# Gate rows of the second block computed as a weight-stationary tile, keys spread by TensorE

## The reference

```python
def hybrid_layer(x, ...):
    h = rmsnorm(x, norm_mix)
    z = h @ w_in                                   # 512 x 1024 times 1024 x 4360
    q_a, k_a, v_a, q_m, k_m, v_m, o_m, if_m, gates = split(z)
    # q_a: 8 heads of 64, k_a and v_a: 2 heads of 64, q_m, k_m: 4 heads of 64,
    # v_m, o_m: 4 heads of 128, if_m: 2 x 4 columns, gates: 2048 columns
    q_a, k_a = partial_rope(rmsnorm(q_a)), partial_rope(rmsnorm(k_a))
    att = sliding_window_attention(q_a, k_a, v_a, sinks)
    i_pre, f_pre = split(if_m + m_gate_bias)       # 4 heads each, 512 tokens
    hm = mlstm_chunkwise(q_m, k_m, v_m, i_pre, f_pre)
    hm = rmsnorm(hm) * sigmoid(o_m)
    mixed = sigmoid(g_a) * (att @ w_att_branch) + sigmoid(g_m) * (hm @ w_m_branch)
    x = x + mixed @ w_out
    u = relu(rmsnorm(x, norm_ffn) @ w_ff1)
    return x + (u * u) @ w_ff2
```

## Time and profile before

| | |
|---|---|
| median of three runs | 3104.98 us |
| the profiled execution | 3104.98 us |
| its span, first to last instruction | 3103.3 us |
| TensorE busy | 3045.1 us, 98% |
| VectorE busy | 1562.1 us, 50% |
| ScalarE busy | 1133.7 us, 37% |
| mean granted TensorE clock | 0.992 |
| ticks 26 to 39 of the second block's first layer | 1761.5 to 1803.6 us |
| the same ticks of its second layer | 2469.2 to 2513.0 us |

### The profile page before, as it was taken

The page is one execution under the profiler, slowest core; times in us unless marked ns, Lnnn a source line. Parts: engine busy times, 40 slices in busy tenths (PEclk is TensorE's granted clock), DMA queues, the critical chain, the costliest instruction groups (busy, mean ns, idle before and its releaser), DMA issues.

```text
span 3103.3 us, 39594 instructions
## 1 busy us (share of the span) xinstructions
PE 3045.1 (98%) x16998; PEld 2549.7 (82%) x16998; DVE 1562.1 (50%) x2145; ACT 1133.7 (37%) x1673; POOL 30.3 (1%) x44
## 2 busy tenths in 40 slices
PE   7999999999999999999999999999999999999999
PEld 6788888887987777888888777898889877798887
DVE  7776654545255465533325654653344654653342
ACT  5555421224233333432224455432232355433231
POOL 0000000000000000000000000000000000000000
PEclk9999999999999999999999999999999999999999
DMA  7433355542332222132322222223222222223322
GB/s 283 156 123 109 109 181 172 168 135 68 95 95 68 69 69 69 46 104 95 95 89 81 82 68 68 82 86 101 98 95 89 82 69 68 82 86 101 99 95 82
DMA packets 219917, 311.59 MB, mean 100 GB/s; under 512 B 12032, under 2 KB 120544, under 8 KB 219744
## 3 DMA queue, kind: packets, MB, share of 16 engines
q1 hardware_dynamic: 208528, 267.01, 26.7%
q0 software_dynamic: 10880, 41.95, 3.8%
q10 hardware_dynamic: 336, 0.12, 0.0%
HBM read 306.93 MB, written 2.10 MB: 100 GB/s over the span
## 4 chain that ended last, share of the span: by engine, by line
PE 88%; DVE 8%; ACT 2%; DMA 1%; issue 1%; ACTq 0%; SPq 0%; DVEq 0%; POOLq 0%
PE G L2065 62%; PE G L2108 8%; PE G L2069 6%; DVE yT L1586 1%; PE X L2161 1%; PE X L2427 1%; DVE w_lo L1235 1%; PE G L2087 1%; PE X L2504 1%; PE G L2227 1%; DMA ada_raw<-in_ada_w 1%; PE X L2488 1%; PE X L2511 1%; DVE hT L1372 1%; DVE yT L1367 1%
## 5 line engine op out<-in xcount | busy, mean ns | idle before, releaser
L2065 PE MATMUL G<-u_hi,w_hi 128*128 128x512 f32 x2160 | 865.5, 401 | 3.3 <-issue 3.2
L2065 PE MATMUL G<-u_hi,w_lo 128*128 128x512 f32 x2160 | 842.7, 390 | 0.0
L2065 PE MATMUL G<-u_lo,w_hi 128*128 128x512 f32 x2160 | 841.3, 389 | 0.0
L1235 DVE TENSOR_TENSOR w_lo<-raw,w_hi 128x2048 fp32r<-128x2048 f32 (+3 forms) x242 | 544.9, 2253 | 501.6 <-ACT w_hi L638 501.0
L638 ACT CAST w_hi<-raw 128x2048 fp32r<-128x2048 f32 (+3 forms) x242 | 454.5, 1880 | 531.8 <-DMA raw<-in_w_ff 242.3
L2065 PEld LDWEIGHTS G<-u_hi,w_hi 128*128 128x128 f32 x2160 | 405.4, 188 | 108.5 <-issue 25.5
L2065 PEld LDWEIGHTS G<-u_hi,w_lo 128*128 128x128 f32 x2160 | 405.4, 188 | 87.8
L2065 PEld LDWEIGHTS G<-u_lo,w_hi 128*128 128x128 f32 x2160 | 406.1, 188 | 79.7 <-issue 1.4
L2065 PE MATMUL G<-ff_hi,w_hi 128*128 128x512 f32 x448 | 174.9, 390 | 0.0
L2065 PE MATMUL G<-ff_hi,w_lo 128*128 128x512 f32 x448 | 174.4, 389 | 0.0
L2065 PE MATMUL G<-ff_lo,w_hi 128*128 128x512 f32 x448 | 174.3, 389 | 0.0
(11 more groups left out here) (425 smaller groups left out, 4341.0 us busy)
## 6 DMA issues: line engine op xcount, KB each, us to landing
raw<-in_w_ff SPq DMA_DIRECT2D x128, 512.0 KB, 4.4
raw<-in_ffn_w_in SPq DMA_DIRECT2D x88, 512.0 KB, 4.5
ada_raw<-in_ada_w POOLq DMA_DIRECT2D x40, 1024.0 KB, 7.2
raw<-in_w_in SPq DMA_DIRECT2D x56, 512.0 KB, 4.4
raw<-in_attn_w_in SPq DMA_DIRECT2D x96, 256.0 KB, 3.7
raw<-in_ffn_w_out SPq DMA_DIRECT2D x40, 512.0 KB, 4.8
raw<-in_hgrn_w_in SPq DMA_DIRECT2D x32, 512.0 KB, 4.7
raw<-in_attn_w_in SPq DMA_DIRECT2D x24, 512.0 KB, 4.5
```

The costliest lines, as they stand in the source:

```text
L1235: tt(w_lo[slot][:, 0:nk, 0:w], raw[slot][:, 0:nk, 0:w], w_hi[slot][:, 0:nk, 0:w].bitcast(F32), ALU.subtract).then_inc(s_lo, 1)
L2065: ins = mm(G[0:c1_ - c0, m, :], w[iw][:, k, c0:c1_], xs[ix][:, x0(b) + kk, :], start=first, stop=last, skip_group_check=True)
```

## The change

The eight `if` columns leave block b = 3, which now has 384 columns, and form the fourth tile of block b = 4. Its weights are 36 columns: i in columns 0 to 3, f in 32 to 35, between them columns of the next matrix part that are computed and not used. So PE makes the two groups of rows directly, in ticks 35 and 39, and the four transposes, the buffer `z_ift`, its clearing by DVE and ACT's copies into it are gone.

The keys are spread by PE: at tick 22 two products with a selecting constant `selk` write both key heads into two banks of PSUM, and ACT copies them at tick 24 in one instruction. PE waits for `k_rotated` at tick 22, ACT for the new `k_spread`. The constant is one more DMA of 128 KB at the start of `at_v` in the first block.

The exponentials stay where they are, in rows, and PE turns i and two exponentials back with three products of 4 columns for each of four token tiles, in place of one product of 68 columns. DVE copies the result in one instruction.

```diff
+    sel = []
+    for kv in range(2):
+        sel.append((r[:, None] // 64 == kv) & (r[:, None] % 64 == r[None, :] % 64))
+    g["selk"] = np.concatenate(sel, 1)
...
         Z_COLUMNS = (z_run((Z["q_a"], 512)), z_run((Z["k_a"], P), (Z["o_m"], P), (Z["q_m"], 256)), z_run((Z["k_m"], 512)),
-                     z_run((Z["v_m"] + 256, 256), (Z["v_a"], P), (Z["if"], 2 * M_HEADS)), z_run((Z["o_m"] + P, 3 * P)))
+                     z_run((Z["v_m"] + 256, 256), (Z["v_a"], P)), z_run((Z["o_m"] + P, 3 * P + GATE_AT)) + [(3 * P + GATE_AT, Z["if"] + M_HEADS, M_HEADS)])
...
                     sp.dma_start(sel4[:, :], a["con2"][:, where2["sel4"][0]:where2["sel4"][1]]).then_inc(s_con, 16)
+                    sp.dma_start(flat(selk[:, :, :]), a["con2"][:, where2["selk"][0]:where2["selk"][1]]).then_inc(s_con, 16)
...
                 elif T == 24:
-                    n.take(ws["k_rotated"])
+                    n.take(ws["k_spread"])
                     n.take(ws["q_scaled"])
-                    for kv in range(2):
-                        for a_ in range(2):
-                            ins = sc.copy(tmp[64 * a_:64 * a_ + 64, kv, :], z_k[64 * kv:64 * kv + 64, 0, :])
-                    n.give(ins, ws["k_ready"])
+                    n.give(sc.copy(tmp[:, 0:2, :], X[:, 0:2, :]), ws["k_ready"])
...
                     n.take(ms["rows"])
-                    sc.copy(cosT[32:32 + M_HEADS, :], z_if[:, 0, :])
-                    sc.activation(cosT[64:64 + M_HEADS, :], row[1], ACT.Exp)
-                    sc.activation(cosT[96:96 + M_HEADS, :], row[3], ACT.Exp, scale=-1.0)
+                    sc.activation(row[1], row[1], ACT.Exp)
                     sc.activation(row[0], row[0], ACT.Exp)
+                    sc.activation(row[3], row[3], ACT.Exp, scale=-1.0)
...
-                            lambda: sc.copy(z_v[:, m, :], G[:, m, 256:256 + P]),
-                            lambda: sc.copy(z_ift[:, m, :].rearrange("p (i c) -> p i c", i=2)[:, :, 0:M_HEADS],
-                                            G[:, m, 3 * P:3 * P + 2 * M_HEADS].rearrange("p (i h) -> p i h", i=2)))
+                            lambda: sc.copy(z_v[:, m, :], G[:, m, 256:256 + P]))
...
                     n.take(ms["columns"])
-                    for i in range(3):
-                        v.tensor_copy(mcol[:, 16 * i:16 * i + 16].rearrange("p (j h) -> p j h", j=TB),
-                                      X[:, 0, 0:272].rearrange("p (j c) -> p j c", j=TB)[:, :, 32 * i:32 * i + M_HEADS])
-                    n.give(v.tensor_copy(mcol[:, 48:80], X[:, 0, 272:304]), ms["columns_copied"])
+                    n.give(v.tensor_copy(mcol[:, :], X[:, 0, 0:80]), ms["columns_copied"])
...
-                    v.memset(z_ift[:, :, :], 0.0)
...
+                elif T == 22:
+                    n.take(ws["k_std"])
+                    n.take(ws["k_rotated"])
+                    for kv in range(2):
+                        ins = mm(X[:, kv, :], selk[:, kv, :], z_k[:, 0, :], start=True, stop=True)
+                    n.give(ins, ws["k_spread"])
...
                 for j in range(TB):
-                    mm(X[:, 0, 68 * j:68 * j + 68], cosT[:, blk(j)], ident[:, 32:100], start=j == 0, stop=True, skip_group_check=True)
+                    mm(X[:, 0, 4 * j:4 * j + 4], gi[:, blk(j)], ident[0:4, 0:4], start=j == 0, stop=True, skip_group_check=True)
+                    mm(X[:, 0, 16 + 4 * j:20 + 4 * j], row[1][:, blk(j)], ident[0:4, 0:4], start=False, stop=True, skip_group_check=True)
+                    mm(X[:, 0, 64 + 4 * j:68 + 4 * j], row[3][:, blk(j)], ident[0:4, 0:4], start=False, stop=True, skip_group_check=True)
...
-                    return [(m, (0, 3 * P + 2 * M_HEADS), (0, 3 * P + 2 * M_HEADS))]
-                return gate_rows if (b, m) == (4, 3) else None
-
-            def gate_rows():
-
-                for j in range(TB):
-                    ins = tr(G[0:GATE_AT + M_HEADS, 3, blk(j)], z_ift[:, j, 0:GATE_AT + M_HEADS], ident)
-                return ins
+                    return [(m, (0, 3 * P), (0, 3 * P))]
+                return (3 * P, 3 * P + GATE_AT + M_HEADS) if (b, m) == (4, 3) else None
```

More of the change, by code:

```diff
@@ L42 @@
 SLOTS = 3
-GATE_AT = 32
 def constants():
@@ L217, in build @@
             cosT, sinT = sb("cosT", [P, S], F32, room), sb("sinT", [P, S], F32, room)
-            sel4, z_ift = sb("sel4", [P, 512], F32, room), sb("z_if_by_token", [P, TB, 2 * GATE_AT], F32, room)
+            sel4, selk = sb("sel4", [P, 512], F32, room), sb("selk", [P, 2, P], F32, room)
         ada_raw = sb("ada_raw", [P, 2, 4, 512])
@@ L294, in build @@
                                              "output", "squares", "variance", "std", "normed", "transposed", "done")}
-        ws = {k: sem("window_" + k) for k in ("q_squares", "k_squares", "q_sums", "k_sums", "q_std", "k_std", "q_scaled", "q_rotated", "k_rotated", "k_ready",
+        ws = {k: sem("window_" + k) for k in ("q_squares", "k_squares", "q_sums", "k_sums", "q_std", "k_std", "q_scaled", "q_rotated", "k_rotated", "k_spread", "k_ready",
                                               "scores", "maximum", "weights", "normalized", "transposed", "copied", "output", "done", "sinks")}
@@ L1643, in rope_tables @@
             def rope_tables():
-                n.take(s_con, 48)
+                n.take(s_con, 64)
                 two_pi = 2 * np.pi
@@ L1843, in mlstm @@
                         bank, i = m_bank(c)
-                        ins = stt(m_state[:, c, :], m_state[:, c - 1, :], mcol[:, 48 + 8 * h + c:49 + 8 * h + c],
+                        ins = stt(m_state[:, c, :], m_state[:, c - 1, :], mcol[:, 32 + 8 * h + c:33 + 8 * h + c],
                                   X[:, bank, (P + 1) * i:(P + 1) * (i + 1)], ALU.mult, ALU.add)
@@ L1853, in mlstm @@
                     link(tt(stat[:, 4:8], den, stat[:, 0:4], ALU.max))
-                    link(tt(stat[:, 4:8], stat[:, 4:8], mcol[:, 32 + h:48:4], ALU.max))
+                    link(tt(stat[:, 4:8], stat[:, 4:8], mcol[:, 64 + h:80:4], ALU.max))
                     link(stt(stat[:, 8:12], stat[:, 4:8], EPS, stat[:, 4:8], ALU.mult, ALU.mult))
@@ L2046, in plain @@
                         last_k = g["ktiles"] - 1
-                        if spec is gate_rows:
-                            if s == g["chunks"] - 1:
-                                ins = gate_rows()
-                                ins.then_inc(s_tile, 1)
-                            else:
-                                ins.then_inc(s_inner, 1)
-                            continue
                         for part in (spec if isinstance(spec, list) else [None]):
@@ L2516, in gate_columns @@
                     return
+                gi = z_if[:, 0, :]
                 n.take(ms["rows_exp"])
@@ L2519, in gate_columns @@
                 for j in range(TB):
-                    mm(X[:, 0, 68 * j:68 * j + 68], cosT[:, blk(j)], ident[:, 32:100], start=j == 0, stop=True, skip_group_check=True)
+                    mm(X[:, 0, 4 * j:4 * j + 4], gi[:, blk(j)], ident[0:4, 0:4], start=j == 0, stop=True, skip_group_check=True)
+                    mm(X[:, 0, 16 + 4 * j:20 + 4 * j], row[1][:, blk(j)], ident[0:4, 0:4], start=False, stop=True, skip_group_check=True)
+                    mm(X[:, 0, 64 + 4 * j:68 + 4 * j], row[3][:, blk(j)], ident[0:4, 0:4], start=False, stop=True, skip_group_check=True)
                 for h in range(M_HEADS):
-                    ins = mm(X[:, 0, 272 + 8 * h:280 + 8 * h], sel4[0:4, blk(h)], srow[:, 6, :], start=False, stop=True, skip_group_check=True)
+                    ins = mm(X[:, 0, 32 + 8 * h:40 + 8 * h], sel4[0:4, blk(h)], srow[:, 6, :], start=False, stop=True, skip_group_check=True)
                 n.give(ins, ms["columns"])
```

1 line of the change is left out of this document (added).

## The result

The changed kernel took 3124.07 us (median of 4 runs, 3123.41 to 3126.72), the kernel before 3105.25 us beside it (4 runs): ratio 1.0062, with a 95% interval of 1.0049 to 1.0075. It is slower by 18.8 us. The forecast was 3118.8 us with a range up to 3123.5, so the direction was right and the time lies outside the range, by 0.6 us. On another chip the same kernel took 3119.36 us against 3106.55, ratio 1.0046 (1.0033 to 1.006); that time lies inside the range. Both intervals hold 1.005, about 15.5 us.

A forecast was written before the change was run, and what follows sets the result against it. TensorE (PE), busy for 98% of the span, was taken as the bound. Per layer 5.06 - 0.24 + 0.10 + 2.00 = 6.92 us, for two layers 13.8, on 3104.98 gave 3118.8 us, range 3114.5 to 3123.5 us.

The forecast's parts named there:

- Gate columns: +2.00 us: Tick 59: 24 small-product instructions at 0.1225 us, less 0.94 for the products replaced; +2.00 us per layer, bounds +1.0 to +3.5.
- the section on the bound: From 1690 to 1810 us PE is busy 117.69 of 120 us at full clock; at most 2.31 us to win per layer.
- the signs that I had named: Tile products at 0.227 to 0.232 us, tick 26 idle under 0.3, tick 59's small products 3.9 us, tick 28 wait 0 to 0.5.
- The spread: Keys spread by PE at tick 22: 1.71 us falls into PE's wait of 1.78 us before tick 26, so 0.
- the layers agree: PE's wait before tick 26 is 1.62 and 1.63 us in the two layers, so one was worked out and doubled.
- The gate tile: Twelve products each into ticks 35 and 39, less the transposes' 0.44 us: +5.06 us per layer, bounds 5.00 to 5.3.
- Block 3: 96 products narrowed from 392 to 384 columns: -0.24 us per layer, bounds -0.32 and 0.
- The late chunk: Block 4's chunk, issued 1.71 us later, may make PE wait before tick 28's scores 0 to 0.5 us; taken +0.1.
- A: Rival, 10%: the spread is not hidden before tick 26, or the late chunk holds up more; 3122.2 us.
- B: Rival, 8%: tick 59's small products cost by their columns, +0.53 in place of +2.00 us per layer; 3115.9 us.
- C: Rival, 3%: PE's time follows few weight columns, the tile costing 1.1 in place of 5.06 us; 3110.9 us, not slower.
- D: Rival, 6%: the longer ticks 35 and 39 take away hidden waits, at most 0.7 us per layer; 3117.4 us.

The follow-up runs named there:

- experiment 6: Kernel before with a filler of 12 more small products (4 rows by 8 columns) at tick 59, results unread: 3117.92 us, ratio 1.0036.
- Experiments 1: The changed kernel without its gate columns, four products of 68 columns back at tick 59: 3115.31 us, ratio 1.003 to the kernel before.
- 2: Kernel before with the new gate columns alone: 3113.45 us, ratio 1.0026.
- 9: Kernel before with 4 more small products (4 rows by 8 columns) at tick 59, results unread: 3108.89 us, ratio 1.0011.
- experiment 7: Kernel before with a wide filler, 4 more plain products of 128 rows and 512 columns at tick 59, results unread: 3113.49 us, ratio 1.0017.
- experiment 4: Kernel before with the keys spread by TensorE alone: 3105.73 us, ratio 1.000.
- 10: Kernel before with the keys spread by TensorE alone, run again on another chip: 3104.28 us, ratio 0.9998.
- experiment 11: The whole change again, on another chip: 3119.36 us, ratio 1.0046 to the kernel before.
- four ticks: The whole change with tick 59's small products spread over ticks 58 to 61: 3119.78 us, ratio 1.0048; run again, 3120.13 us, ratio 1.0041.
- experiments 5: The whole change with tick 59's small products split over ticks 59 and 60: 3121.75 us, ratio 1.0046 to the kernel before.

## Why the prediction was wrong

**The step that failed is "Gate columns: +2.00 us".** It counted the small products' own time, 24 x 0.1225 less 0.94, and took for granted what the section on the bound said of the clock, "at the full clock". That row is of a stretch ahead of tick 59, without a single product of 4 rows. The products' own term came out at 1.77. The 0.23 between are in the row that I took the price from: its 0.98 us for eight instructions hold the step to the next kind of product. Inside a run the same products, of 4 rows by 8 columns, take 2.70 / 24 = 0.1125 us (experiment 6). What was missing is what they do to the stream behind them: they bring the granted clock from 2.4 to 1.2 GHz for about 3.4 us, or twice that in two of twelve layers, which costs 1.5 to 3.2 us per layer. Experiments 1 and 2 put the fall on this part of the change, 6 and 9 make it in the kernel before with small products alone, 7 shows that wide ones don't. Why small products bring the clock down is not shown. None of the signs that I had named looked at the clock.

**The spread.** Predicted 0, and it is 0 in ticks 11 to 26 (experiments 4 and 10). But my working stopped at the wait. In no layer with the wait filled did the clock fall behind it, which gives 1.56 us back in a layer in which it would have fallen. By 7 in 12 layers that is 0.9 us per layer; the traces say so, the times of experiments 4 and 10 can't tell it from none. I had the trace to see it: the time from tick 26 to tick 34 was 24.65 in one layer and 26.21 in the other, but "the layers agree" rested on the wait alone.

**The gate tile.** Predicted 5.06, measured 5.10; the 0.228 us per product lies in the 0.227 to 0.232 named. The price of 128 weight columns held for 36, so the time follows what streams.

**Block 3.** -0.24 predicted, -0.25 measured, in part by luck. I had given all of it to the 72 products behind tick 26 and nothing to the 24 before. Behind it 24.65 became 24.48, -0.17. The other 0.08 came before tick 26 (11.48 us from tick 22 became 11.40), where I had said that they only lengthen a wait: with the spread no wait was left.

**The late chunk.** +0.1 predicted, 0 measured in this execution, and 0.07 and 0.12 in two of twelve layers. ACT's rounding began 1763.61 - 1758.83 = 4.78 us behind the issue, in the lower half of my 4.24 to 5.6.

**The rivals.** A (spread not hidden) did not happen: no idle time at tick 26. B (price by columns) would have been 1.47 us for the 24 instructions; they took 2.71, as many of 8 columns 2.70. C (price by weight columns) is out by the tile's 2.73 us for twelve. D (hidden waits) is out: ticks 40 to 56 are the same to 0.02 us. None of the four priced the clock.

**The sum.** The terms that I priced measure 2 x 6.64 = 13.3 us where I had 13.8. The clock adds, in the mean of the four layers of the two executions, 3.81 - 1.77 = 2.04 per layer and takes off 0.93 at tick 26: +1.1, in all 2 x 7.75 = 15.5 us. The intervals of both measurements hold this. So the clock at these two places, 2.2 us in the mean, is less than half of the 5.0 us by which the first measurement (+18.8) exceeds the forecast (+13.8). In its profiled execution, of 3123.32 us, it came to 3.3 us, with the long fall in the second layer. On the second chip the forecast of +13.8 looks met, with +12.8; as the same falls are in that trace, this is luck. The range was too narrow because its ends came from the sizes of priced terms and the spread of runs, and the clock was no term.

The rest of the first measurement most likely is the clock elsewhere. Its thirteen recorded executions had a mean granted clock of 0.9886, the five of experiment 11 one of 0.990. Among the thirteen, the slowest (3128.87 us) had 0.987 and the fastest (3120.44 us) 0.990. Only one of them is traced, so where the others lost their time is not shown.

**What stays open.** Where the first measurement's other executions lost the 3 us above the sum; why the fall began early, and was twice as long, in two of twelve layers; why it comes behind tick 26 in 7 of 12 layers, with the same wait; whether 4 rows or few columns make the small products count; and whether four ticks gain the 1.8 us in the time that their trace shows.

## What to carry to other kernels

Price a run of tiny products by the stream behind it too: read the granted clock there, in every layer, and take the price of a fall from any row of the kernel that has one. The same look belongs to each short wait of PE: work put into a wait may be worth more than nothing, as here no fall came behind a filled wait. Where such products are needed, keep each run short (0.98 us brought no fall here, 1.88 us did) or merge them into wider ones, as the kernel before had with 68 columns; cutting a run up costs something of its own (0.24 us per added change of kind here), which may eat the gain. Take the price of one instruction from inside a run of its kind, not from a row that ends with the step to the next kind. And where a time comes out some us off, compare the granted clock in the parts that the change doesn't touch before you explain it.

## What the runs showed of the hardware that was not expected

- The granted clock fell to 1.2 GHz while PE, by the profile's count, was busy for 100% of the stretch, behind 1.88 to 3.7 us of products of 4 rows (experiments 5, 6, 9), and did not behind 3.58 us of plain products of 128 rows and 512 columns (experiment 7). The Trainium skill, "TensorE: Matmul & The Clock Gate", section "HAM oscillation — how this bites in real kernels", puts the fall down to gaps in which PE is idle between its products. The 1.62 us of wait before tick 26 are a gap, though a shorter one than the waits that the page describes, and were followed by a fall in 7 of 12 layers; behind tick 59 the traces disagree with the page, as the profile shows no gap there.
- A short fall costs nearly the same each time: 1.55 to 1.65 us (experiments 6, 9, 11 and the whole change), at half clock for 3.4 us.
- Plain products of 4 rows cost the same with 4 and with 8 columns: twenty-four instructions of 4 by 4 took 0.113 us each (the whole change), as many of 4 by 8 0.1125 (experiment 6). The 0.1225 of the earlier trace rows is the price of the last eight of a run, with the step to the next kind in it.
- Four plain products of 512 columns in a row took 3.58 us, 0.45 per instruction; I had expected 2.6 to 2.7, though the two of tick 11 already took 1.71 us for four instructions.
- Half clock isn't rare in this kernel, and not the same from one execution to the next: ahead of tick 11 of the first layer it lasted from 44 us (spread alone, experiment 4) to 65 us (experiment 6) in the fourteen traces.
